# One dot in four handed from VectorE to GpSimd and ScalarE in the down pass of an expert layer

## The reference, cut to what matters

```python
u = expert_down[idx]                                   # (tokens, heads, 16, 1024)
act = gelu(einsum('thkd,td->thk', u, xb))              # one dot of length 1024 per picked expert
v = expert_up[idx]
out = einsum('thk,thkd->td', softmax_weight * act, v)
```

## Time and profile before

| | |
|---|---|
| median of 3 runs | 4268.2 us (4265.16 to 4270.73) |
| profiled execution, its own time | 4266.67 us |
| its span, first to last instruction | 4264.9 us |
| mean granted TensorE clock | 0.969 |
| busy: TensorE matmul, weight load | 94%, 78% |
| busy: VectorE, ScalarE, GpSimd | 60%, 39%, 41% |
| down pass in the trace | from about 1890 us to 3155 us |

### The profile page before, as it was taken

One profiled execution on the slowest core, in us unless ns is written; L12 is line 12 of the kernel. 1 busy time (PEld: TensorE's weight loads), 2 busy tenths in 40 slices (PEclk: granted clock), 3 DMA queues, 4 the chain that ended last, 5 costly groups with the idle time before them and its releaser, 6 DMA issues. The chain is left out here.

```text
span 4264.9 us, 62088 instructions
## 1 busy us (share of the span) xinstructions
PE 3990.5 (94%) x22397; PEld 3317.1 (78%) x22428; DVE 2542.5 (60%) x4790; ACT 1654.5 (39%) x3214; POOL 1759.6 (41%) x1278
## 2 busy tenths in 40 slices
PE   8899999989799788989999999999969999999998
PEld 3688887768677677979999999999956776766776
DVE  3455411145566623669999999997665555555555
ACT  1123333334422242113777777777722222122122
POOL 0233333335433402213333333335447666666664
PEclk9999999989899898989999999999989999999999
DMA  7223333234355333237788888889999998999987
GB/s 297 56 79 98 99 103 99 89 107 131 113 162 189 113 104 108 69 101 255 239 271 274 278 266 283 273 271 352 346 326 346 334 330 323 328 327 334 333 327 279
DMA packets 637600, 939.49 MB, mean 220 GB/s; under 512 B 198692, under 2 KB 416180, under 8 KB 637364
## 3 DMA queue, kind: packets, MB, share of 16 engines
q1 hardware_dynamic: 319412, 408.93, 29.3%
q0 software_dynamic: 110592, 402.70, 26.7%
q10 hardware_dynamic: 207360, 124.80, 9.4%
HBM read 790.55 MB, written 145.75 MB: 220 GB/s over the span
## 5 line engine op out<-in xcount | busy, mean ns | idle before, releaser
L1874 POOL DMA_INDIRECT down_rows<-in_peer_down_dram,row_ids x384 | 457.0, 1190 | 848.5 <-DVE row_u L2014 755.5
L1895 PE MATMUL p_u<-h2T_hi,downT_hi 128*128 128x320 f32 x2048 | 655.1, 320 | 11.1 <-ACT gelu_out L1945 10.4
L1895 PE MATMUL p_u<-h2T_lo,downT_hi 128*128 128x320 f32 x2048 | 635.1, 310 | 0.0
L1895 PE MATMUL p_u<-h2T_hi,downT_lo 128*128 128x320 f32 x2048 | 634.7, 310 | 0.0
L2014 DVE CUSTOM_DVE_ANT_0 gate_rows<-down_rows,x_tok_rows 128x1024 f32<-128x1024 f32 x384 | 468.9, 1221 | 89.0 <-DMA down_rows<-in_peer_down_dram,row_ids 74.8
L2170 POOL DMA_INDIRECT up_rows<-in_peer_up_dram,row_ids_turned x384 | 415.3, 1082 | 241.3 <-PE p_rows L2333 146.2
L2372 PE MATMUL p_y<-up_hi,coef_hi 128*128 128x512 f32 x1240 | 494.8, 399 | 1.1 <-DVE coef_lo L2267 1.1
L2372 PE MATMUL p_y<-up_lo,coef_hi 128*128 128x512 f32 x1240 | 485.5, 392 | 0.0
L2372 PE MATMUL p_y<-up_hi,coef_lo 128*128 128x512 f32 x1240 | 482.7, 389 | 0.0
L2277 DVE TENSOR_TENSOR y_acc<-p_y,y_acc 128x512 f32<-128x512 f32 x310 | 211.3, 690 | 374.6 <-PE p_y L2372 374.6
L514 PE MATMUL p<-hT_hi,w_hi 128*128 128x512 f32 x1024 | 405.0, 395 | 0.0
(11 more groups left out here) (349 smaller groups left out, 7953.5 us busy)
## 6 DMA issues: line engine op xcount, KB each, us to landing
down_raw<-in_peer_down_dram SPq DMA_DIRECT2D x128, 512.0 KB, 5.7
up_raw<-in_peer_up_dram SPq DMA_DIRECT2D x128, 512.0 KB, 5.9
scratch_gu<-gelu_out ACTq DMA_DIRECT2D x128, 320.0 KB, 5.1
gelu_in<-scratch_gu SPq DMA_DIRECT2D x128, 320.0 KB, 4.3
weights_in<-scratch_w SPq DMA_DIRECT2D x128, 320.0 KB, 6.7
w_raw<-in_w_in_dram SPq DMA_DIRECT2D x64, 512.0 KB, 4.1
w_ada_sb<-in_w_ada_dram SPq DMA_DIRECT2D x12, 2048.0 KB, 15.1
scratch_w<-weights_out ACTq DMA_DIRECT2D x40, 512.0 KB, 7.6
```

The costliest lines, as they stand in the source:

```text
L1874: pool.indirect_dma_start(out=rows[:, c % RING, :], out_offset=None, in_=inp["peer_down"][0], in_offset=bass.IndirectOffsetOnAxis(ap=row_i ...
L1895: mm = pe.matmul(ps_u[half][:, 0:HD], d[:, n % 3, k, :], h2[h][:, k, half * HD:(half + 1) * HD], start=(j == 0), stop=(j == 3 * KD - 1))
```

## The change

Row blocks with `c % 4 == 3` no longer go to VectorE. GpSimd multiplies them with the tokens in place, and ScalarE sums them by an Identity activation with an accumulator. The other three quarters stay on VectorE. The number of row blocks per tile changes as well: 279 in the first 98 tiles (2.85 a tile) and 3.5 a tile in the last 30, 105 in all. GpSimd's product of row block `c - 2` stands on its queue ahead of fetch `c`, for `c % 4 == 1`; the last one stands behind the last fetch. ScalarE's sum of a row block stands in the tile of `dots_of`, behind `first` and ahead of `select_act` and `store_weights`. Fetch `c` with `c % 4 == 3` waits for ScalarE's sum of `c - 4`.

```diff
+        row_product, row_summed = m.sem("row_product_done"), m.sem("row_summed")
...
-        LATE_DOTS = (E1 - LATE) * 4
+        LATE_DOTS = (E1 - LATE) * 7 // 2
...
-            return range(early + (n - LATE) * 4, early + (n - LATE + 1) * 4)
+            return range(early + (n - LATE) * 7 // 2, early + (n - LATE + 1) * 7 // 2)
+
+
+        def vector_dots(c):
+
+            return c - (c + 1) // RING
...
+                def product(c):
+                    pool.wait_ge(rows_loaded[c % RING], 16 * (c // RING + 1))
+                    pool.tensor_tensor(rows[:, c % RING, :], rows[:, c % RING, :], x_tok[:, c // P], ALU.mult
+                                       ).then_inc(row_product, 1)
+
                 for c in range(TA):
...
-                    if c >= RING:
-                        pool.wait_ge(dot_done, c - RING + 1)
+                    if c >= RING and c % RING == RING - 1:
+                        pool.wait_ge(row_summed, c // RING)
+                    elif c >= RING:
+                        pool.wait_ge(dot_done, vector_dots(c - RING) + 1)
+                    if c >= RING and c % RING == 1:
+                        product(c - 2)
                     pool.indirect_dma_start(out=rows[:, c % RING, :], out_offset=None, in_=inp["peer_down"][0],
...
+                product(TA - 1)
...
+                def sum_row(c):
+                    a, k = divmod(c, P)
+                    act.wait_ge(row_product, c // RING + 1)
+                    act.activation(rows[:, c % RING, :], rows[:, c % RING, :], ACT.Identity, accum_out=row_u[:, a, k:k + 1]
+                                   ).then_inc(row_summed, 1)
...
                     for g in granules_of(n + 1):
                         first(g)
+                    for c in dots_of(n):
+                        if c % RING == RING - 1:
+                            sum_row(c)
                     for head in ended_in(n):
...
-                        dve.wait_ge(dot_done, c)
+                        dve.wait_ge(dot_done, vector_dots(c))
...
-                    todo = dots_of(n)
+                    todo = [c for c in dots_of(n) if c % RING < RING - 1]
```

## The result

The changed kernel takes 4483.23 us (median of 4 runs, 4479.88 to 4485.31) against 4268.28 us before: 215 us slower, ratio 1.0502 (95% interval 1.0489 to 1.0514). The forecast was 4295 us, with a range to 4350. The direction was right, the size was not; the nearest of the cases written down was the serial chain through ScalarE at 4356 us, and it too was far too small.

A forecast was written before the change was run, and what follows sets the result against it. VectorE was taken to bound the first 98 tiles of the down pass, TensorE the last 30. The terms -69 + 84 + 8 + 5 = +28 us on the profiled 4266.67 gave 4295 us, range 4225 to 4350.

The forecast's parts named there:

- the serial chain through ScalarE: Down pass, rival: ScalarE waits at sums for late products, delaying Gelu and copy behind; 4356 us, chance 0.18.
- dots leave VectorE: First 98 tiles: 55 fewer dots on VectorE at 1.25 us each, -69 us; TensorE's idle time allows 54.
- products meet VectorE: First 98 tiles: 70 GpSimd products stall VectorE's instructions with two SBUF inputs, 1.2 us each, +84 us (0 to 168).
- ScalarE's sums: First 98 tiles: 70 sums of about 1.15 us on ScalarE, busy 75%, lengthen VectorE's copy waits: +8 us (0 to +50).
- the ring: First 98 tiles: fetch-to-fetch loop of buffer 3 takes 9.85 us where 14.0 are there; holds on average, no cost.
- VectorE as the bound, TensorE next: First 98 tiles: VectorE sets the pace at 10.0 us a tile; TensorE's idle time caps the gain at 54 us.
- The shared port: First 98 tiles: a GpSimd product holds up VectorE's two-SBUF-input instructions, 1.2 us a product, +84 us in all.
- The last 30 tiles and the tail: End of down pass: rows set the pace at 11.15 us a loop, +2; late weight stores +3; together +5 us.
- the lock is seldom met: First 98 tiles, rival: products fall in VectorE's selection, costing 0.4 us each; 4226 us, chance 0.24.
- Its first sign: Down pass, sign of the serial chain through ScalarE: ScalarE waits several us before the sums.

The follow-up runs named there:

- the dropped fourth: Changed kernel with every fourth row block fetched but neither multiplied nor summed, its buffer free once the row has landed; a quarter of the dots left out: 4233.82 us.
- the free product: As the dropped fourth, plus a same-size GpSimd product on other tensors that waits for no row and nobody awaits; VectorE's dots write in place: 4306.01 us.
- the free sum: As the dropped fourth, plus a same-size ScalarE sum over another tensor, waiting for no row; dots write in place: 4264.57 us.
- complete kernel with two buffers: Changed kernel, nothing left out, GpSimd's rows alternating between two buffers, product just ahead of the next fetch of its kind, dots in place: 4341.18 us.
- The spread: Kernel before with only the new number of dots per tile, all dots staying on VectorE: 4272.58 us.
- the second buffer: Changed kernel with GpSimd's rows alternating between two buffers, dots in place, product at its early place two fetches behind its own fetch: 4383.47 us.
- Moving the product: Changed kernel with the product of row c - 4 just ahead of fetch c, not two fetches after its own: 4400.90 us with one buffer.
- the memsets: As the free product, but with two 128x1024 GpSimd memsets in place of the product, reading nothing in SBUF: 4239.56 us.

## Why the prediction was right or wrong

The terms for the first 98 tiles, against the stretches of the runs (the dropped fourth against the kernel before, the free product and the free sum against the dropped fourth; the ring is what is left of the changed kernel's stretch):

| first 98 tiles | prediction | measured |
|---|---|---|
| dots leave VectorE | -69 | -21 |
| products meet VectorE | +84 | +61 |
| ScalarE's sums | +8 | +29 |
| the ring | 0 | +64 |
| together | +23 | +133 |

*VectorE as the bound, TensorE next: half right.* Dropping the fourth does make the kernel faster, but by 33 us, of which 21 are in the first 98 tiles. The term for those was -69, of which I had myself found only 54 to be had, and the sum nevertheless took 69. The bound behind VectorE is ScalarE as much as TensorE: `low` waits 169 us for its copy.

*The shared port: the term held.* 1.2 us a product was taken from the layout of two tiles, between 0 and 2.4. The free product stretched VectorE by 1.27 us each. In the changed kernel itself it is 89 us for 96 products, 0.9 each; in the complete kernel with two buffers 122 us, again 1.27 each. In time the free product costs 61 us in the first 98 tiles, where the sum had 84. The stretching is not only in instructions with two SBUF inputs, as it was priced, but also in casts and `tensor_scalar` (below): in the changed kernel the dots have only 26 of the 89 us.

*ScalarE: the term was mis-sized.* +8 was written for the first 98 tiles, 29 was measured there (31 in all). The prediction named the DMA issues that the 75% do not count and gave them no price. That ScalarE's idle time lies in front of waits, where it is not room for a sum, is the likely reason; no run separates it.

*The spread: right, and small.* +17 us in the first stretch and -12 behind it, +5.6 in all.

*The ring: the step that failed.* The prediction said that the loop is 9.85 us for four rows where 14.0 are there, that "on average it holds", and that in the last 30 tiles it is 11.15 us. The starts in the trace of the changed kernel, as means over its loops, give:

| | first 98 tiles | last 30 tiles | prediction |
|---|---|---|---|
| fetch issued to product | 6.8 | 7.0 | 5.9, 7.2, and 0.2 |
| product | 2.45 | 2.5 | 2.4 |
| product done to start of sum | 4.75 | 1.5 | 0.2, with the row of the next fetch |
| sum | 1.15 | 1.15 | 1.15 |
| sum done to next fetch | 0.8 | 1.5 | in that 0.2 |
| loop | 15.9 | 13.7 | 9.85, 11.15 |

The services were right. What was missing is the turn: the product ends in the midst of ScalarE's tile, and the sum comes where ScalarE's order has it; it ends while GpSimd stands at another wait or issues the two fetches ahead of this one. In the last 30 tiles it is mostly the latter: one product ends at 3326.62, its sum starts at 3326.66, and the fetch goes at 3330.11, behind two others. The mean of 4.75 us in the first stretch is partly slack, since the whole tile had become longer (15.9 us is 1.4 tiles of 11.4). That the loop nevertheless binds there is shown by the second buffer: 81 of its 100 us are in the first 98 tiles (1104.4 to 1023.8), where the prediction had put nothing. The sentence that behind the product stand the next fetches was there too, but no price: while GpSimd waits for a landing, VectorE's own rows are not fetched. Moving the product shows that price. It is in the last 30 tiles and the tail: 63 us with one buffer and 58 with two. In the first 98 tiles the move gave 24 us with one buffer and took 21 with two. So it was the turn on ScalarE that failed "on average it holds", and the product's wait that failed the last 30 tiles.

*The parts add up, in part by chance.* The fourth dropped 4233.8, the port and GpSimd's queue +72.2, ScalarE's time +30.8: 4336.8. The complete kernel with the chain loosened: 4341.2. With the chain: 4483.2. That the first two agree within 5 us is better than the parts deserve: in the first 98 tiles they give 1040, and the kernels with two buffers took 1024 to 1045.

*The last 30 tiles and the tail: wrong by 81 us.* +5 had been written, +86 came. The rows do set the pace there, as said, but at a loop of 13.7 us instead of 11.15: landing and product are as priced, the two handovers take 3.0 us instead of 0.2. 26.25 such loops are 360 us, and the stretch took 358. Behind it come ScalarE's last weight stores, which stand behind the last sum: in the changed kernel ScalarE waited 10.13 us for the last product and only then issued them, tail 21.3 us.

```profile
3364.58 1.06 ACT L2003 ACTIVATE down_rows<-down_rows 128x1024 f32<-128x1024 f32 x1 [10.13 <-POOL down_rows L1876]
3364.58 1.36 ACTq L1997 DMA_DIRECT2D scratch_w<-y_acc  x2
```

*The rivals and the signs.* The sign that was written down for "the lock is seldom met" came true: the mean dot is 1290 ns in 2050 to 2850 and 1309 in the whole pass, under 1.35 us. It was a bad sign, because it looked at the dots alone; over all instructions a product cost VectorE 0.9 us in the changed kernel, not the 0.4 of that rival. The chain was the nearest mechanism, with chance 0.18 and a price of +74 us over the first terms; loosening it gave 142. It was priced as a delay of single sums on ScalarE, with Gelu and copy behind them. Its first sign came true: ScalarE waits 4.3 us on the mean before 31 sums. The other did not: TensorE's waits for Gelu are 43 us and VectorE's for the copy 91 in the whole pass, not hundreds. That the chain goes through GpSimd's queue to VectorE's rows (274 us of waits) was left out. What the lower granted clock adds was not measured by itself; it follows the waits and goes with them (0.94 in 2050 to 2850 with the chain, 0.96 with two buffers).

## What to carry to other kernels

A wait on an in-order queue holds up everything behind it, and costs as much as what is behind it has no slack: before work is put on the engine that issues the fetches, ask for how long it will stand there and whose data are not fetched meanwhile. In a ring that goes round through three in-order engines, the loop is not the sum of the services but takes in each engine's turn; one more buffer is the cheap cure, and should be in the change from the start. Where such work should stand on the fetching queue depends on the stretch: here the late place paid where landings set the pace and cost 21 us where they did not. A kernel with two buffers that has the product early in the first 98 tiles and late in the last 30 was not built; by the stretches above one estimates some 20 us less than 4341 for it, still no gain. And price first what the relief is worth if the moved work were free: here it was 33 us, and the sum on ScalarE alone, 31 us, already took it back.

## What the runs showed of the hardware

A running elementwise product on GpSimd stretches more of VectorE's work than instructions with two SBUF inputs. In the run with the free product a cast of 128x32 from SBUF to SBUF took 680 ns on the mean instead of 204 without the product (183 in the kernel before), and up to 2280 where it met one. With two buffers the `TENSOR_SCALAR` of 128x16 took 940 instead of 175. MAX8 is not stretched: 28 of the 98 of line 1436 ran wholly within a product of GpSimd there, and none of the 98 took more than 298 ns (mean 286, before 286):

```profile
L1466 DVE TENSOR_SCALAR down_sel_ij<-down_sel_ci 128x16 uint32<-128x16 uint32 x49 | 46.1, 940 | 1.7
...
L1436 DVE MAX8 down_sel_top<-down_sel_scores_rest 128x8 f32<-128x128 f32 x98 | 23.9, 286 | 1.7
```

The prediction had no row for MAX8 under a GpSimd instruction; this is one. A memset on GpSimd, which only writes, left the dots at 1220 ns and stretched the cast to 413. So one kind of VectorE instruction meets GpSimd's reads, another its writes too. The Trainium skill, page "SBUF — State Buffer", section "Who interferes with whom", names copies, casts and `tensor_scalar` as those that can take the whole shared pair, and two-input instructions as those that meet only reads; these rows agree. One row fits neither kind: FIND_INDEX8 of 128x256 behind that cast (line 1458) took 509 ns on the mean beside the memsets and 414 without them.
